# Half-size weight units in four half slots, beside the expert gathers of a two-block layer

## The reference, cut to what matters

```
qry = (xt @ w_query).reshape(T, H, 2, 128)                 # 8 heads
s = einsum('thpd,phnd->thpn', qry, sub_keys)               # top 16 of each half, then top 16 of the pairs
u  = expert_down[ib];  act = gelu(einsum('td,thkd->thk', xb, u))
vv = expert_up[ib];    y   = einsum('thk,thkd->td', gb * act, vv)
```

## Time and profile before

| | us |
|---|---|
| median of 3 runs | 3343.16 |
| the three runs | 3343.91, 3334.45, 3343.16 |
| the profiled execution, its own time | 3332.33 |
| its span in the profile | 3330.5 |
| TensorE busy | 2957.0 (89%) |
| VectorE busy | 1236.3 (37%) |
| GpSimd busy | 733.7 (22%) |
| ScalarE busy | 544.5 (16%) |
| bytes read | 1203.41 MB, 362 GB/s over the span |

### The profile page before, as it was taken

The page is one execution under the profiler, slowest core; times in us unless marked ns, Lnnn a source line. Parts: engine busy times, 40 slices in busy tenths (PEclk is TensorE's granted clock), DMA queues, the critical chain, the costliest instruction groups (busy, mean ns, idle before and its releaser), DMA issues.

```text
span 3330.5 us, 23847 instructions
## 1 busy us (share of the span) xinstructions
PE 2957.0 (89%) x8013; PEld 1297.7 (39%) x8013; DVE 1236.3 (37%) x1894; ACT 544.5 (16%) x1292; POOL 733.7 (22%) x598
## 2 busy tenths in 40 slices
PE   8999997898988999997688878887699989999999
PEld 4444443343443443443233333333254533333344
DVE  1100014452354343345666755544532133222220
ACT  1110001111121110112213211211122111001010
POOL 1000002332234222233444434433400000000000
PEclk9999999899999999999898998999889989999999
DMA  9878887998989999999999999999967749999982
GB/s 351 307 273 295 306 300 294 412 394 345 408 352 406 422 412 404 409 404 401 421 411 405 417 419 418 417 419 419 416 231 268 259 186 422 422 422 422 422 309 76
DMA packets 266321, 1206.77 MB, mean 362 GB/s; under 512 B 14912, under 2 KB 17520, under 8 KB 162928
## 3 DMA queue, kind: packets, MB, share of 16 engines
q1 hardware_dynamic: 191872, 668.08, 52.1%
q0 software_dynamic: 74352, 537.48, 39.3%
HBM read 1203.41 MB, written 2.10 MB: 362 GB/s over the span
## 4 chain that ended last, share of the span: by engine, by line
PE 52%; DMA 34%; issue 4%; DVE 4%; DVEq 2%; POOL 2%; SPq 1%; ACT 1%; ACTq 0%; POOLq 0%
DMA W<-in_peer_expert_down,big 15%; PE bank L926 14%; DMA W<-in_w_expert_up 8%; PE bank L995 7%; DMA W<-in_w_in 7%; PE bank L1479 6%; PE bank L917 5%; PE bank L1089 5%; PE bank L1586 4%; PE bank L1644 3%; DMA W<-in_w_peer_query 2%; DVEq L2393 1%; DMA XS<-in_peer_expert_up,big 1%; DVE W L2543 1%; PE bank L1570 1%
## 5 line engine op out<-in xcount | busy, mean ns | idle before, releaser
L2543 DVE CUSTOM_DVE_ANT_0 W<-W,big 128x2048 f32<-128x2048 f32 x256 | 585.7, 2290 | 603.4 <-DMA W<-in_peer_expert_down,big 602.0
L855 POOL DMA_INDIRECT W<-in_peer_expert_down,big x256 | 357.2, 1395 | 1043.8 <-issue 503.6
L1479 PE MATMUL bank<-XT,big 128*128 128x512 f32 x488 | 270.3, 705 | 121.5 <-ACT big L1927 115.1
L1479 PE MATMUL bank<-XS,big 128*128 128x512 f32 x536 | 263.8, 638 | 70.6 <-DMA XS<-in_peer_expert_up,big 46.8
L926 PE MATMUL bank<-W,XT 128*128 128x512 f32 x704 | 310.8, 600 | 5.9 <-DMA W<-in_w_peer_query 5.9
L1479 PE MATMUL bank<-W,big 128*128 128x512 f32 x512 | 241.6, 616 | 46.3 <-ACT big L1927 43.9
L1089 PE MATMUL bank<-W,XT 128*128 128x512 f32 x480 | 220.8, 615 | 37.6 <-DMA W<-in_w_in 37.6
L1919 ACT ACTIVATE small<-small 128x1 f32<-128x1 f32 x256 | 51.7, 202 | 1161.3 <-DVE small L2543 1148.5
L1586 PE MATMUL bank<-W,XS 128*64 128x512 f32 x1024 | 226.5, 596 | 14.2 <-DMA W<-in_w_expert_up 11.6
L864 POOL DMA_INDIRECT XS<-in_peer_expert_up,big x130 | 185.5, 1427 | 195.0 <-PE bank L1479 156.4
L917 PE MATMUL bank<-W,XT 128*128 128x512 f32 x480 | 211.0, 597 | 3.8 <-DMA W<-in_w_in 3.8
(11 more groups left out here) (376 smaller groups left out, 2689.5 us busy)
## 6 DMA issues: line engine op xcount, KB each, us to landing
W<-in_w_in SPq DMA_DIRECT2D x132, 2048.0 KB, 13.0
W<-in_w_expert_gate SPq DMA_DIRECT2D x68, 1024.0 KB, 15.0
W<-in_w_expert_up SPq DMA_DIRECT2D x68, 1024.0 KB, 17.0
W<-in_w_out SPq DMA_DIRECT2D x32, 2048.0 KB, 8.8
big<-in_w_expert_down SPq DMA_DIRECT2D x32, 2048.0 KB, 12.5
W<-in_w_ret_branch SPq DMA_DIRECT2D x16, 2048.0 KB, 8.2
W<-in_w_peer_query SPq DMA_DIRECT2D x16, 2048.0 KB, 10.7
W<-in_w_attn_branch SPq DMA_DIRECT2D x8, 2048.0 KB, 10.4
```

The costliest lines, as they stand in the source:

```text
L855: pool.indirect_dma_start(down_row(n), None, down_t, row).then_inc(down_in[n % DOWN_ROWS], 16)
L1479: mm = pe.matmul(bank[4 * (n // P) + c][:, :], DIAG[:, m % 4, :], up_row(n)[:, c * CH:(c + 1) * CH], start=n % P == 0, stop=n % P == P - 2)
L2543: dve.tensor_tensor_reduce(out=down_row(n), in0=down_row(n), in1=HN[n // P], scale=1.0, scalar=0.0, op0=ALU.mult, op1=ALU.add, accum_out=d ...
```

## The change

Between the same two points of the order the weights come in units of 1 MB. The memory of slots 0 and 1 is divided into four half slots, each with one of the four load semaphores. A load waits for the last unit before it that used the same memory or the same semaphore. The 108 units become 216 half units; all bytes, all matmuls, the rings of the gathers and the picks that VectorE adds stay. The lengths of the contiguous runs in memory stay too (2, 4 or 8 KB).

```
-    order += [("query", 0, c, half) for c in range(4) for half in range(2)]
-    order += [("in1", 1, g, j) for g in range(8) for j in range(2 if g == 1 else 4)]
+    order += [("query", 0, c, j) for c in range(4) for j in range(4 if c else 2)]
+    order += [("in1", 1, g, j) for g in range(8) for j in range(4 if g == 1 else 8)]
     for name in WIDE:
-        order += [(name, 1, j) for j in range(4 if name == "att" else 8)]
-    order += [("in2", 0, g, j) for g in range(5) for j in range(4)]
+        order += [(name, 1, j) for j in range(8 if name == "att" else 16)]
+    order += [("in2", 0, g, j) for g in range(5) for j in range(8)]
...
-TWO_SLOTS, FOUR_AGAIN = INDEX["query", 0, 1, 0], INDEX["in2", 1, 0, 0]
+HALVES, WHOLE_AGAIN = INDEX["query", 0, 1, 0], INDEX["in2", 1, 0, 0]
...
+def places_of_units():
+    places, landed, earlier, signals = [], [], [], [0] * SLOTS
+    for i in range(len(ORDER)):
+        half = HALVES <= i < WHOLE_AGAIN
+        s = (i - HALVES if half else i - WHOLE_AGAIN if i >= WHOLE_AGAIN else i) % SLOTS
+        lo, hi = (2048 * s, 2048 * (s + 1)) if half else (UNIT * s, UNIT * (s + 1))
+        there = [j for j in range(i) if places[j][0] == s or places[j][1] < hi and lo < places[j][2]]
+        signals[s] += 16
+        places.append((s, lo, hi))
+        landed.append(signals[s])
+        earlier.append(there[-1] if there else None)
+    return places, landed, earlier
...
-    for i in range(4):
-        key = ("query", 0, 2 + i // 2, i % 2)
-        when[key] = int(i * 2.3)
+    for i in range(8):
+        key = ("query", 0, 2 + i // 4, i % 4)
+        when[key] = int(i * 1.15)
...
-        when[key] = at + i if i < 6 else int(at + 6 + (i - 6) * 1.25)
+        when[key] = at + i // 2 if i < 12 else int(at + 6 + (i - 12) * 0.625)
...
-            when[key] = int(at + i * 1.1)
+            when[key] = int(at + i * 0.55)
             put(pe, when[key], *key)
         x = when[units[-1]]
-        at = max(at + len(units) * 1.1, x + 2)
+        at = max(at + len(units) * 0.55, x + 2)
...
-        start, pace, hop = (134, 4, 1) if t == 0 else (261, 1, 0)
+        start, pace, hop = (134, 2, 1) if t == 0 else (261, 1, 0)
```

In `wide_unit` a half unit is one block against the four banks, and in `paired_unit` two blocks against two banks:

```
-                for c, k in [(c, k) for c in range(4) for k in range(2)] if first or last else [(c, k) for k in range(2) for c in range(4)]:
+                for c in range(4):
...
-                    for k in range(4):
+                    for k in range(2):
```

More of the change, by code:

```diff
@@ L61 @@
 WIDE = ("gate_a", "gate_r", "att", "ret", "mix", "query")
-OUT2 = [[("out2", 0, g, j) for g in range(2) for j in (2, 3, 0, 1)],
+OUT2 = [[("out2", 0, g, j) for g in range(2) for j in (4, 5, 6, 7, 0, 1, 2, 3)],
         [("out2", 1, c, half) for half in (1, 0) for c in range(4)]]
@@ L65 @@
 INDEX = {key: i for i, key in enumerate(ORDER)}
-TWO_SLOTS, FOUR_AGAIN = INDEX["query", 0, 1, 0], INDEX["in2", 1, 0, 0]
+HALVES, WHOLE_AGAIN = INDEX["query", 0, 1, 0], INDEX["in2", 1, 0, 0]
 UG = INDEX["ple", 0]
[L68 to L74, removed]
+def places_of_units():
[10 more added lines that the diff above has]
+    return places, landed, earlier
+PLACES, LANDED, EARLIER = places_of_units()
+SLOT = [place[0] for place in PLACES]
 def rows_of_up():
@@ L685, in source @@
                 if kind == "in1":
[L686 to L696, removed]
+                    w, at = w_in, IN1[key[2]][0]
+                elif t == 1 and kind in WIDE:
+                    w, at = wide_from[kind], 0
+                elif kind == "query":
+                    w, at = w_q, CH * key[2]
+                elif t == 0 and kind == "in2":
+                    w, at = w2, col[CHUNK_E[2 * key[2]][0]]
+                elif t == 0 and kind == "out2":
+                    w, at = w_out2, 1024 * key[2]
+                else:
+                    w, at = None, 0
+                if w is not None:
+                    n, ks = columns(key), depth(key)
+                    return w.rearrange("(k p) n -> p k n", p=P)[:, ks * key[-1]:ks * key[-1] + ks, at:at + n]
                 if kind == "in":
@@ L742, in _ @@
                 load(i)
-            sp.wait_ge(w_used, INDEX["ret", 1, 7] + 1)
+            sp.wait_ge(w_used, INDEX["ret", 1, 15] + 1)
             sp.dma_start(HN[1], A["ffn_norm"].to_broadcast([P, D])).then_inc(grow_loaded, 16)
-            for i in range(INDEX["query", 1, 0], INDEX["in2", 0, 0, 2]):
+            for i in range(INDEX["query", 1, 0], INDEX["in2", 0, 0, 4]):
                 load(i)
@@ L924, in unit @@
                 pe.wait_ge(w_loaded[SLOT[i]], LANDED[i])
-                for k in range(8):
-                    mm = pe.matmul(out, lhs(k), slot(i)[:, k, :], start=first and k == 0, stop=last and k == 7)
+                ks = depth(key)
+                for k in range(ks):
+                    mm = pe.matmul(out, lhs(k), slot(i)[:, k, :], start=first and k == 0, stop=last and k == ks - 1)
                 mm.then_inc(w_used, 1)
@@ L980, in wide_unit @@
             def wide_unit(name, j):
-                i, count = INDEX[name, 1, j], 4 if name == "att" else 8
+                i, count = INDEX[name, 1, j], 8 if name == "att" else 16
                 first, last = j == 0, j == count - 1
@@ L1028, in query_unit @@
                 if c == 0:
-                    pe.wait_ge(kept1, 2 + 2 * half)
-                unit(("query", 0, c, half), query_out(0, c)[:, :], lambda k: xt(8 * half + k, 0), half == 0, half == 1)
+                    pe.wait_ge(kept1, 2 + 2 * j)
+                ks = 4 if c else 8
+                unit(("query", 0, c, j), query_out(0, c)[:, :], lambda k: xt(ks * j + k, 0), j == 0, ks * j + ks == KC)
             def turn_query(t, c):
@@ L1079, in in1_unit @@
                 at, width = IN1[g]
-                ks = 4096 // width
+                ks = depth(("in1", 1, g, j))
                 i = INDEX["in1", 1, g, j]
@@ L1333, in _ @@
             for c in range(2):
-                query_unit(c, 0)
-                query_unit(c, 1)
+                for j in range(4 if c else 2):
+                    query_unit(c, j)
                 turn_query(0, c)
```

59 lines of the change are left out of this document (29 added, 30 removed).

## The result

The changed kernel takes 3297.64 us (median of 4 runs, 3293.73 to 3301.08) against 3341.95 us of the kernel before in the same comparison: a ratio of 0.9871, 95% interval 0.9851 to 0.9892, 44 us less. The forecast was 3321 us with a range from 3289 to 3352: the direction was right, and the gain is twice the 22 us of the sum.

The account below looks back on a forecast made before the run. The prediction took the picks to be bound by the bytes the DMA engines move; gains of 13 (in1), 6 (WIDE), 2 (query) and 1 us (tile 1's picks) made 22, so 3343.2 - 22 = 3321 us, range 3289 to 3352.

Parts of the forecast that it names:

- What bounds the kernel: From about 540 to 2400 us, DMA bytes bound the picks; against a 420 GB/s ceiling, at most 69 us can be gained.
- I take the middle: In in1 and WIDE, about half the shortfall is recovered: 13 of 26.7 us and 6 of 12.4.
- earlier slots: Half slots free 3.4 us sooner and TensorE begins with 1 MB landed; over all stretches this gains 22 us.
- From 960 to 1000 us ... 0: Retention stretch, ticks 45 to 53: no unit stands, VectorE and TensorE wait for each other; gain 0, bounds 0 and 10.8.
- Tile 1's picks, 1 us: 1680 to 2400 us: units come every fourth tick from slots long full; smoother load gains 1 of 6.9 us.
- the last step moves two ticks: 0: Beside tile 1's picks the last step moves from tick 242 to 244 of 256, its tail inside the picks; cost 0.
- The base of the sum: The 22 us were taken from the profiled 3332.3 us and equally from the median, 3343.2 us, giving 3310 and 3321.
- Costs taken at 0: 108 more loads and waits, the 1 MB size, the moved order and choose(4), in time by one tick, cost 0.
- the sum is 0: WIDE ending at tick 111 instead of 104 gains nothing, as bytes bound both WIDE and the pure ticks behind it.
- full recovery: Rival: DMA engines stay full in in1, WIDE and the query stretch; 54 us gained, 3289 us; chance 0.15.
- Hidden anyway: Rival: weights land sooner and gathers later by the same bytes, so only a few us move; 3340 us, chance 0.27.
- starved: Rival in WIDE and in1: more weights in flight delay down gathers and VectorE; +20 us, 3363 us; chance 0.18.

Follow-up runs that it names:

- e14: e1 with a half slot's load held until both halves of the pair there have been used; 3303.95 us, 0.9884 of the kernel before.
- e15: e1 with TensorE waiting at a pair's first half until both halves have landed; 3306.49 us, 0.9897 of the kernel before.
- e13_both_held: e1 with slots freed only by pairs and TensorE waiting for both halves to land; 3345.72 us, 1.0009 of the kernel before.
- e6: The changed kernel with only the ticks beside tile 1's picks put back to those of before; 3292.54 us, 0.9851 of the kernel before.
- e1: The changed kernel with every half unit at its whole unit's tick and other steps at their old ticks; 3291.92 us, 0.9855 of the kernel before.
- e2_order: The kernel before, 2 MB units in two slots, but at the changed kernel's ticks; 3325.16 us, 0.9954 of the kernel before.
- e11_less_in1: The kernel before with each in1 unit loading three quarters of its columns, all matmuls kept; 3322.28 us, 0.9937 of the kernel before.

## Why the prediction was wrong

The shortfall to 420 GB/s, by the same formula as in the prediction, from the windows above:

| stretch | shortfall before | after | recovered | predicted |
|---|---|---|---|---|
| query | 7.4 | 90 x 38/420 = 8.1 | -0.7 | 2 |
| in1 | 26.7 | 335 x 15/420 = 12.0 | 14.7 | 13 |
| retention | 10.8 | 45 x 21/420 = 2.3 | 8.5 | 0 |
| `WIDE` | 12.4 | 510 x (-1)/420 = -1.2 | 13.6 | 6 |
| 1520 to 1680 us of before | 5.0 | 150 x 8/420 = 2.9 | 2.1 | 0 |
| tile 1's picks | 6.9 | 720 x 7/420 = 12.0 | -5.1 | 1 |
| sum | 69.2 | 36.1 | 33.1 | 22 |

The windows' borders do not lie at the same picks. Cut at the same picks, in1 recovers 17.3 us, retention 8.2 and `WIDE` 11.0, and the sum stays 33. It fits the 31.2 us between the two profiled executions. So of the 22 us by which the gain of 44 passed the forecast, some 9 to 11 are terms of the sum and 13 its base. The steps that failed are the middle taken for `WIDE`, the 0 for the retention stretch, and the sum carried over from the profiled execution to the median. Step by step:

*What bounds the kernel* was right. The bytes did: the gain in the traces is the recovered shortfall. The chain named the pattern that the change removes.

*"I take the middle"* in the step on earlier slots is the first term that was mis-sized. For in1 it came near (13 against 15 to 17). For `WIDE` it was half of what came: 6 against 11 to 14, all that there was. The reason given, that no row tells the two apart, treated the step as one mechanism that might work or not. e14 and e15 show two, each of which alone fills `WIDE` (419 GB/s), while in in1 each recovers about a third and both together two thirds.

*"From 960 to 1000 us ... 0"* is the second, and the one whose reason was wrong. The premise was that no unit stands there. But a unit of in1 runs from 958.53 to 967.49 us and the last one from 971.66 us, and VectorE's wait, which ends at 968.42 us, lasted as long as it did because TensorE had waited 8.02 us for the first of the two. With half slots VectorE's wait is 10 us shorter, and 8 us of shortfall went.

*Tile 1's picks, 1 us*, and *"the last step moves two ticks: 0"*: the shift cost 5 to 6 us by the traces, near pick 160. I looked only at whether the end of the list stayed inside the picks, not at what stands at the ticks between.

*The base of the sum.* The remaining 13 us (44 - 31) lie between the profiled executions and the medians. I moved the sum over to the median as if the distance were the same before and after. It was 9.6 us on one side for the kernel before (its profile shows an execution of 3332.33 us, its medians are 3340 to 3344 in all comparisons) and 3.4 us on the other side for the changed kernel. Where the two executions fell was chance. For the 9.6 us, e13_both_held is the nearest thing to a second look: it is about as fast as the kernel before (1.0009) and its profiled execution took 3344.64 us. Its windows of in1, retention and `WIDE`:

```profile
620.00:965.00 345.00, 303.96 (x744) 137.85 (x743) 136.93 (x188) 55.54 (x146) 96.46 (x67) 0.94 0.97 385
965.00:1005.00 40.00, 33.08 (x83) 16.25 (x82) 21.98 (x39) 11.76 (x23) 15.36 (x9) 0.88 0.74 281
1005.00:1535.00 530.00, 478.95 (x1094) 208.73 (x1093) 202.05 (x224) 69.72 (x195) 152.49 (x115) 0.96 0.99 403
```

The shortfalls are 345 x 35/420 = 28.8, 40 x 139/420 = 13.2 and 530 x 17/420 = 21.5, 63.5 us in all against 49.9 in the rows that I had. The table by picks has it 13.5 us behind the profiled execution of before at pick 128. So a slower execution can have some 13 us more of just the shortfall that the change recovers. This is shown for e13, which is another kernel; that the ordinary executions of the kernel before have it too is inferred, as there is one trace of it.

*Costs taken at 0*: smaller loads (e13: none found), the waits between units, and `choose(4)` in time by one tick all held; the gathers show no gap before pick 128. The order's seven ticks, "the sum is 0", held for half units (e6 against e1) and not for whole ones (-16 in e2_order).

*The rivals.* The full recovery (3289) was the nearest of the cases, at 0.15, though its 54 us were not recovered: the traces show 33, and the base did the rest. "Hidden anyway" had VectorE's waits for down rows as its reason, and they did grow from 217.7 to 278.8 us, while the time fell: such waits are what a kernel looks like when its bytes bound it. Of "starved" only the growth came: the DMA share in `WIDE` is 1.01, where it needed less than 0.97. The fixed cost of about 2.0 us that the Trainium skill gives a DMA ("DMA: Bandwidth & Descriptors", section "Anatomy of one DMA", fitted there to DMAs that GpSimd issues) would be 216 us for 108 more loads, an estimate, if it stood one behind another. These loads are SyncE's, and e13_both_held bounds them at 0.2% of 3340, 7 us or 0.06 us each, where several are in flight.

## What to carry to other kernels

Where transfers bound a stretch, cut it into stages and take (1 - rate / ceiling) of each as what can be won; if a change offers two ways to keep the queue filled, either alone may already win all of it, as in `WIDE`, or they may add, as in in1. Look also behind the stretch: an engine that comes late out of it makes the next one pay. Halving the piece over the same 4 MB was worth 49 us at no memory, and halving it again in query and in1 nothing; but a quarter of the memory less took two thirds of that away. Smaller pieces need their order checked as well: two halves with other work between them hold memory longer if they are freed together, and steps moved by rounding may meet others. Two versions with half units and unmoved ticks beside tile 1's picks (3291.9 and 3292.5 us) had the lowest medians of all that read every byte.

## What I had not expected of the hardware

108 further loads, with the same bytes in pieces of 1 MB instead of 2 MB, are not measurable (1.0009, 0.9999 to 1.002). A load of three quarters of the bytes did not land in time either: in1's last but one unit was waited for 8.46 us in e11_less_in1 and 8.02 us in the kernel before. And two equally fast kernels, with the same instructions but for the split loads and waits, show the queue running dry to different degrees in the executions that were traced: 403 GB/s in `WIDE` in one of 3344.64 us, 410 in one of 3332.33.
